# Layer 0's convolution and MLA branches and output product as three fp32r passes, MLA heads in step

## The reference

```
def _merge_branches(pt, ys, p):
    g_a, g_b, g_c = jnp.split(jax.nn.sigmoid(pt[10]), 3, axis=-1)
    return (g_a * ys[0] + g_b * ys[1] + g_c * ys[2]) @ p['w_out']

def _attend(qn, qr, kn, kr, v):            # MLA: 8 heads, 128 + 64 wide
    s = (einsum('bhqd,bhkd->bhqk', qn, kn) + einsum('bhqd,bkd->bhqk', qr, kr)) * MLA_SCALE
    return einsum('bhqk,bhkd->bhqd', softmax(s), v)

def _trunk_layer(...):
    parts = split((x * (1 + scale1) + shift1) @ w_in + b_in)
    y = merge(gla(parts), attend(...) @ mla_wo, conv_module(parts) @ conv_wo)
    x = layer_norm(DN_ALPHA * x + gate1 * y)
    x = layer_norm(DN_ALPHA * x + gate2 * conv_ffn(x * (1 + scale2) + shift2))
```

## Time and profile before

| | us |
|---|---|
| median of three runs | 3217.84 (3217.02 to 3219.92) |
| the profiled execution | 3218.65 |
| its span | 3216.8 |
| PE busy | 3022.4 |
| DVE busy | 1681.4 |
| ACT busy | 1160.4 |

### The profile page before, as it was taken

How to read it: one execution, slowest core, us unless ns; L and a number is a source line. 1 busy time by engine, 2 the same in 40 slices (tenths; PEclk the granted TensorE clock), 3 DMA queues, 4 the chain that set the end, 5 groups by cost and what they waited for, 6 DMA issues and landing times.

```text
span 3216.8 us, 40794 instructions
## 1 busy us (share of the span) xinstructions
PE 3022.4 (94%) x16475; PEld 2287.7 (71%) x16475; DVE 1681.4 (52%) x2885; ACT 1160.4 (36%) x1911; POOL 273.6 (9%) x146
## 2 busy tenths in 40 slices
PE   6989899999998989999999999999999899898998
PEld 3666554444444468877588866789988898897997
DVE  4148867642221177753538882249753644545554
ACT  2033420133231153332323133347555444434444
POOL 2000000000000000000000000000020333320442
PEclk8999999999999999999999999999999999989999
DMA  6223324322323222332223442245652564432562
GB/s 210 79 66 92 92 66 153 122 69 92 104 93 119 90 79 92 99 93 73 89 56 92 126 113 79 92 144 191 177 174 66 151 179 143 143 100 76 166 176 91
DMA packets 419325, 362.38 MB, mean 113 GB/s; under 512 B 20229, under 2 KB 392550, under 8 KB 419140
## 3 DMA queue, kind: packets, MB, share of 16 engines
q1 hardware_dynamic: 416928, 359.11, 36.1%
q10 hardware_dynamic: 1028, 0.39, 0.0%
q0 software_dynamic: 1184, 0.28, 0.0%
HBM read 358.70 MB, written 1.05 MB: 112 GB/s over the span
## 4 chain that ended last, share of the span: by engine, by line
PE 79%; DVE 9%; ACT 5%; issue 4%; DMA 2%; POOL 0%; SPq 0%; POOLq 0%; DVEq 0%; ACTq 0%
PE banks L1037 16%; PE banks L878 7%; PE banks L827 7%; PE banks L910 6%; PE banks L912 5%; PE banks L911 5%; PE banks L901 3%; PE banks L1293 3%; PE banks L1284 3%; DVE conv_out L2503 2%; PE banks L1068 1%; PE banks L1000 1%; ACT narrow_hi L1535 1%; PE banks L1002 1%; PE banks L1001 1%
## 5 line engine op out<-in xcount | busy, mean ns | idle before, releaser
L2293 DVE TENSOR_TENSOR narrow_lo<-wring,narrow_hi 128x1024 fp32r<-128x1024 f32 (+1 forms) x212 | 268.9, 1271 | 379.0 <-ACT narrow_hi L1535 378.8
L910 PE MATMUL banks<-operand_narrow,narrow_hi 128*128 128x256 f32 x1312 | 392.3, 299 | 39.7 <-DVE operand_narrow L2825 20.7
L1535 ACT ACTIVATE narrow_hi<-wring 128x1024 fp32r<-128x1024 f32 (+2 forms) x312 | 309.0, 998 | 223.4 <-PE banks L912 139.7
L911 PE MATMUL banks<-operand_narrow,narrow_hi 128*128 128x256 f32 x1312 | 377.0, 287 | 0.0
L912 PE MATMUL banks<-operand_narrow,narrow_lo 128*128 128x256 f32 x1312 | 377.0, 287 | 0.0
L797 POOL TENSOR_TENSOR narrow_lo<-wring,narrow_hi 128x1024 fp32r<-128x1024 f32 x100 | 251.0, 2513 | 1434.1 <-ACT narrow_hi L1535 1434.1
L2503 DVE SCALAR_TENSOR_TENSOR conv_out<-conv_in,vectors,conv_out 128x512 f32<-128x512 f32 (+1 forms) x464 | 286.6, 618 | 15.3
L910 PEld LDWEIGHTS banks<-operand_narrow,narrow_hi 128*128 128x128 f32 x1312 | 257.7, 196 | 49.2 <-issue 27.8
L1037 PE MATMUL banks<-operand_a,wring 128*128 128x512 f32 (+1 forms) x768 | 256.3, 489 | 3.9 <-DMA wring<-in_w_in_dram 3.9
L911 PEld LDWEIGHTS banks<-operand_narrow,narrow_hi 128*128 128x128 f32 x1312 | 257.7, 196 | 1.7
L912 PEld LDWEIGHTS banks<-operand_narrow,narrow_lo 128*128 128x128 f32 x1312 | 257.4, 196 | 0.0
(11 more groups left out here) (376 smaller groups left out, 5795.9 us busy)
## 6 DMA issues: line engine op xcount, KB each, us to landing
wring<-in_w_in_dram SPq DMA_DIRECT2D x52, 1024.0 KB, 5.4
wring<-in_w_ada_dram SPq DMA_DIRECT2D x48, 1024.0 KB, 5.7
wring<-in_ffn_wup_dram SPq DMA_DIRECT2D x44, 1024.0 KB, 5.1
wring<-in_w_ff_in_dram SPq DMA_DIRECT2D x32, 1024.0 KB, 5.4
wring<-in_w_ff_out_dram SPq DMA_DIRECT2D x32, 1024.0 KB, 5.7
wring<-in_ffn_wdown_dram SPq DMA_DIRECT2D x32, 704.0 KB, 4.7
wring<-in_w_in_dram SPq DMA_DIRECT2D x36, 512.0 KB, 5.1
wring<-in_w_in_dil_dram SPq DMA_DIRECT2D x18, 1024.0 KB, 5.0
```

The lines of the kernel that those rows point to most:

```text
L910: pe.matmul(out, wh, a[:, 0:SEQ], start=first, stop=False)
L911: pe.matmul(out, wh, a[:, SEQ:512], start=False, stop=False)
L1535: act.activation(dst, src, f, **kw).then_inc(*inc)
L2293: tt(NL[:, v % 4, 0:kn, :], w, NH[:, v % 4, 0:kn, :].bitcast(F32), ALU.subtract).then_inc(ev("narrow_lo"), 1)
```

## The change

The gates and values of `co0` and `mo0` and the product `wout0`, 40 tiles in all, become units like those of `up0`: three fp32r passes each. For that ACT makes high parts of `AF` (`MXH`, written where `X` lay), of the convolution's output (`COH`), of MLA's output (`MOH`) and of the merged output (`AH`), and DVE the low parts (`MXL`, `COL`, `MOL`, `GLO`). `X` is saved to device memory by a DMA on POOL's queue once `AF` is made, and comes back when the last gate of `mo0` is done. The highs and lows of the weights get slots of their own for each stage (`SLOTS`, `OVERLAP`, `unit_slot`); ACT and DVE make one unit's split and low at each filler tile, in front of which the units counted so far must be done.

In MLA (both layers) units go in pairs of two heads for the same queries. PE writes both `QN` products, then both `QR` products, the one on rows 0 to 63, the other on rows 64 to 127; then come both turnings, the next pair's scores, the fillers, and both values. DVE's order within a pair is: the next pair's softmax, the fillers, then both copies of the values.

`keep_clock` issues products whose result is overwritten: five in front of layer 1's first tiles, four at `kt` in each layer, six in front of `up0`, three or four at `up1`, `sqk` and `dqk`, two at each of the two `ffin`.

```
     def unit_slot(u):
-        return u if u < 3 else (u - 3) % 2
+        branch, mix_out, up = (pl.unit_at[pl.first[name]] for name in ("co0.1", "wout0", "up0"))
+        if u < branch:
+            return 3 + u
+        if u < mix_out:
+            return 6 + (u - branch) % 2
+        if u < up:
+            return 8 if (u - mix_out) % 2 == 0 else 6
+        i = u - up
+        return 9 + i if i < 3 else (i - 3) % 2
...
# POOL
+        pool.wait_ge(ev("operand_a"), KD)
+        pool.dma_start(XD, X[:, :, :].rearrange("p k n -> p (k n)")).then_inc(ev("x_saved"), 16)
+        pool.wait_ge(ev("x_saved"), 16)
+        pool.wait_ge(*done(pl.last("mo0.6")))
+        pool.dma_start(X[:, :, :].rearrange("p k n -> p (k n)"), XD).then_inc(ev("x_back"), 16)
...
# PE
+        def product3(t, hi, lo, ready=None):
+            u = pl.unit_at[t]
+            pe.wait_ge(ev("w_lo"), u + 1)
+            start_tile(t)
+            wh, wl = unit_parts(u)
+            for k in range(KD):
+                if ready:
+                    ready(k)
+                pe.matmul(bank(t), wh[:, k, :], hi(k), start=k == 0, stop=False)
+                pe.matmul(bank(t), wh[:, k, :], lo(k), start=False, stop=False)
+                mm = pe.matmul(bank(t), wl[:, k, :], hi(k), start=False, stop=k == KD - 1)
+            mm.then_inc(*made(t))
...
+        def keep_clock(t, n):
+            for _ in range(n):
+                pe.matmul(bank(t), cn("ones"), CN[:, 0:512], start=True, stop=True)
...
         # first_tiles(n, ready, *names, idle=0), after arrived / w_lo waits of all its tiles
+            keep_clock(tiles[0][0], idle)
             for k in range(KD):
                 ready(k)
...
             def scores(u):
...
+                for j in range(2):
+                    t, h = F[f"m{l}.s{u + j}"], mla_unit(u + j)[0]
+                    start_tile(t)
+                    pe.matmul(bank(t, 0, nk), QN[:, h, i], KN[:, h, c0:512], start=True, stop=False)
+                for j in range(2):
+                    t, h = F[f"m{l}.s{u + j}"], mla_unit(u + j)[0]
+                    r = slice(64 * j, 64 * j + 64)
+                    mm = pe.matmul(bank(t, 0, nk), QR[h // 2][r, i], KR[r, c0:512], start=False, stop=True)
...
+            start_tile(F[f"kt{l}"])
+            keep_clock(F[f"kt{l}"], 4)
...
-            cols(f"wout{l}", KD, G, n, lambda k: pe.wait_ge(ev("merged_out"), KD * (2 * l + 1) + k + 1))
+                for m in range(KD):
+                    product3(F["wout0"] + m, lambda k: AH[:, k, :], lambda k: GLO[:, k, :],
+                             None if m else lambda k: pe.wait_ge(ev("out_lo"), k + 1))
...
-                first_tiles(n, a_ready(), ("up0", 2))
+                first_tiles(n, a_ready(), ("up0", 2), idle=6)
...
# DVE, after kr0
+            if l == 0:
+                for m in range(KD):
+                    dve.wait_ge(ev("mix_hi"), m + 1)
+                    tt(MXL[:, m, :], AF[:, m, :], MXH[:, m, :].bitcast(F32), ALU.subtract).then_inc(ev("mix_lo"), 1)
+                lows(1)
...
# DVE, MLA
+            softmax(0)
+            for u in range(0, n_units, 2):
+                if u + 2 < n_units:
+                    softmax(u + 2)
+                for name, q in fillers[u // 2]:
                     filler(name, q)
+                if l == 0 and u >= 22 and u % 4 == 2:
+                    mla_low((u - 22) // 2)
+                    mla_low((u - 22) // 2 + 1)
+                value(u)
+                value(u + 1)
...
# DVE, residual after wout0 and the layer norm's end
-                if l == 0 and m == KD - 1:
-                    lows(1)
+                if l == 0 and m:
+                    lows(n_low[0])
...
-                        lows(2)
+                        lows(n_low[0])
+                        lows(n_low[0])
```

More of the change, by code:

```diff
@@ L378, in branch_phase @@
             pl.gemm(f"{name}.{h}", [(cols_chunk(wo if h % 2 else win, (0 if h % 2 else c0) + h // 2 * 256), 2)],
+                    split=lambda i: name in ("co0", "mo0"),
                     after=(lambda j: ada_slot(name[:2] == "wo" and j)) if name[2:] == "0" and (name != "co0" or h)
@@ L828, in parts, with branch_split, conv_split, mla_split @@
             mm.then_inc(*made(t))
+        def product3(t, hi, lo, ready=None):
[10 more added lines that the diff above has]
+            mm.then_inc(*made(t))
+        def branch_split(name, hi, lo, ready, halves):
+            for half in halves:
+                for j in range(2):
+                    t = F[f"{name}.{half}"] + j
+                    if half % 2:
+                        product3(t, hi, lo, ready if half == 1 and j == 0 else None)
+                    else:
+                        product3(t, lambda k: MXH[:, k, :], lambda k: MXL[:, k, :],
+                                 (lambda k: pe.wait_ge(ev("mix_lo"), k + 1)) if name == "co0" and half + j == 0 else None)
+                    if name != "co0" or half:
+                        ada_slot()
+                    yield
+        def conv_split(halves):
+            return branch_split("co0", lambda k: COH[:, conv_tile(k), :], lambda k: COL[:, k, :],
+                                lambda k: pe.wait_ge(ev("conv_lo"), k + 1), halves)
+        def mla_split(halves):
+            return branch_split("mo0", lambda k: MOH[:, k, :], lambda k: MOL[:, k, :],
+                                lambda k: pe.wait_ge(ev("mla_lo"), k + 1), halves)
         def cols_a(name, n, skip=0):
@@ L1229, in mla @@
                 yield
[L1230 to L1236, removed]
+                for j in range(2):
+                    t, h = F[f"m{l}.v{u + j}"], mla_unit(u + j)[0]
+                    pe.wait_ge(*freed(F[f"m{l}.t{u + j}"]))
+                    start_tile(t)
+                    for i in range(nk // P):
+                        mm = pe.matmul(bank(t, 0, P), VM[:, c0 // P + i, h * P:(h + 1) * P],
+                                       PT[:, j, i * P:(i + 1) * P], start=i == 0, stop=i == nk // P - 1)
+                    mm.then_inc(*made(t))
         for l in range(2):
             n = toks(l)
-            first_tiles(512, a_ready(), (f"gr{l}", 1), *([(f"k{l}", 2)] if l else []))
+            first_tiles(512, a_ready(), (f"gr{l}", 1), *([(f"k{l}", 2)] if l else []), idle=5 * l)
             pe.wait_ge(*freed(F[f"gr{l}"]))
@@ L1355, in _ @@
             fillers = mla_fillers(l)
[L1356 to L1359, removed]
+            if l:
+                todo = {"co": branch("co1", CV, n, lambda k: pe.wait_ge(ev("conv_ready"), KD + k + 1), range(1, KD)),
+                        "mo": branch("mo1", B, n, None, (0, 2, 4, 6))}
+            else:
+                todo = {"co": conv_split(range(1, KD)), "mo": mla_split((0, 2, 4, 6))}
+            for pair, _ in enumerate(mla(l)):
+                for name, q in fillers[pair]:
                     next(todo[name])
@@ L1379, in _ @@
             if l == 0:
-                run(narrow_cols("sqk", a_ready(), squares(F["mpre0"])))
+                run(narrow_cols("sqk", a_ready(), squares(F["mpre0"]), 3))
                 row_scale(0)
@@ L1919, in _ @@
                 op(dst, bank(t), ACT.Copy, free(t))
+                if l == 0 and 4 <= i < 10:
+                    conv_high(i - 4)
+                if l == 0 and 10 <= i < 12:
+                    split(i - 8)
+            if l == 0:
+                conv_high(6)
+                conv_high(7)
             n_units = 16 * len(sets[l])
@@ L1964, in _ @@
                      {5: lambda: narrow(up1, 0), 6: lambda: narrow(up1 + 1, 0), 7: lambda: narrow(up1 + 2, 0)} if l else
-                     {6: lambda: split(up), 7: lambda: split(up + 1)})
+                     {m: lambda: split(n_split[0]) for m in range(1, KD)})
             if l:
@@ L2666, in _ @@
             n_units = 16 * len(sets[l])
+            if l == 0:
+                for m in range(KD):
+                    dve.wait_ge(ev("conv_hi"), m + 1)
+                    tt(COL[:, m, :], CV[:, m, :], COH[:, conv_tile(m), :].bitcast(F32), ALU.subtract)\
+                        .then_inc(ev("conv_lo"), 1)
+                    if m == 5:
+                        lows(3)
             def maxima(u):
```

176 lines of the change are left out of this document (119 added, 57 removed).

## The result

The changed kernel takes 3163.26 us (median of four runs, 3161.41 to 3167.2), against 3217.43 for the kernel before in the same comparison: a ratio of 0.9833, 95% interval 0.9816 to 0.985. Forecast were 3161, range 3126 to 3198. The profiled execution took 3165.07 us, its span is 3163.2; that is 53.6 less than the profiled execution of before, where 56.9 were forecast. One later execution, the one that was profiled of the run with the dummies in front, was disturbed (3435.46 us at a mean granted clock of 0.83), so no row of that run is read.

What follows compares the result with a forecast made beforehand. PE was taken as the bound: busy 94% of the span, carrying 79% of the chain. Gains of MLA, mo0, wout0 and smaller terms, less losses at up0 and gr1, sum to -56.9 us: 3161 from the median, range 3126 to 3198.

Steps and rivals of the forecast that it cites:

- The passes: 40 tiles as three fp32r passes: 5.44 us each, saving 1.43 a tile beside nothing, 1.62 in the MLA stage.
- MLA of layer 0: Layer 0's MLA stage: paired heads and cheaper filler tiles, less new waits for value copies; 34 us gained (25 to 55).
- unit of 256 keys: Layer 0's MLA: PE time of one unit at 256 keys before the change, put at 1.96 us.
- up0's start: Between wout0 and up0's body: late weight lows, then six dummies behind that wait; 15.5 us lost (14.5 to 18.5).
- layer 1's first tiles: Layer 1's start (gr1): five dummies stand behind the chunk wait, costing 6.6 us and saving 2.3; 4 us lost.
- kt: Four dummies fill 3.4 us of a 5.40 us hole in each layer: 2 us gained per layer, 4 together.
- `co0`'s first two tiles: Cheaper passes save 2.9 us, but PE waits about 2.8 for the first low: 0 (bounds -3 and +4).
- The MLA of layer 1: Eight 64-row products vanish (8.4 us), a first pair's softmax costs about 2.4: 6 us gained (bounds -9 and +8).
- Covered waits: Rival: waits for value copies in layer 0's MLA pairs are covered, 21.5 us more gained, 3140; chance 0.16.
- A fallen clock: Rival: PE's clock falls after the MLA pairs' waits, 3.1 us at each of 15 pairs, 3208; chance 0.08.
- The dry ring: Rival: late slot release makes 11 MLA-stage weight chunks each cost a wait and half clock, 86 us lost, 3248; chance 0.05.
- No gain in the passes: Rival: with lows or loads between them tiles stay near 6.87 us, 57 us not gained, 3219; chance 0.03.

Runs made afterwards that it cites:

- the run with all three: Changed kernel plus up0's weight lows made early, dummies of two starts before their waits, value copies before lows in layer 0's MLA: 3124.11 us, ratio 0.9725.
- the run with the products apart: Changed kernel with each head's 64-row score product again following its own 128-row product: 3195.51 us, ratio 0.9946 to the kernel before.

## Why the prediction was right

**The passes.** 1.4 us a tile came out: wout0 43.7 us for 54.95, eight tiles. In the MLA stage it was 1.41 too (7.06 less 5.65), not 1.62. The values of `mo0` take 47.9. The wait of 4.70 for weights is gone there; that it is gone because the ring slots are now freed by the low was not tested by itself. (A tile is 24 matmuls in its three passes; the 48 in the prediction's signs is a slip.)

**MLA of layer 0, -28.9 for -34.** The idle time is as counted: 240 - 213.8 = 26.2 us in the window, forecast 21.5 + 4.5. The order of DVE as its cause is shown by the run with the values first. That the waits sum to 21.3 for 21.5 is partly luck. Three of the 14 hold 5.5 us that the prediction did not count: a table load of 1.28 us on ACT in front of a sigmoid (the wait before 897.68), the lows of two finished heads, 1.20 us each time (before 911.69 and 946.07), and 1.83 us for which ACT waits for a late chunk (before 946.07). The chain behind that last one, the longest:

```profile
936.94 5.16 DMA wring<-in_w_in_dram
942.13 1.06 ACT branch_w_hi L1640
943.29 1.23 DVE branch_w_lo L2443
944.51 1.20 DVE mla_out_lo L2836 x2
```

The missing 5 us are busy time, 213.8 for 207.8: a filler tile takes 5.65 on the mean of 22 and not 5.44, since its first products, behind other shapes, come slower than 0.227 (4.6 us together; at 803.66 the second follows the first after 0.34), and one pair's scores ran at half clock, 1.6 us. The step that was mis-sized is the filler's price, which I had taken from up0's unbroken row of tiles. The prediction's unit of 256 keys, 1.96, is a slip too: its own terms add up to 1.88, 1.4 us less over the eight pairs.

**up0's start, +16.0 for +15.5, and layer 1's first tiles, +4.3 for +4.** Both causes are shown by edits: the first by the lows made early alone (16 us back), the second by the dummies in front of the wait, read in the run with all three (6.3 back).

**The small ones.** kt gave more than taken, 3.3 and 3.6 for 2 each, as the states behind it ran at full clock too. `co0`'s first two tiles gave 0.4 for 0. The MLA of layer 1 gave 4.3 for 6 although a pair saves more than I took (9.9 by the products, 9.3 in the run with them apart): the first softmax and the values behind the merges must then cost 5.0 to 5.6, not 2.4; this split was not measured. X's way out and back took 7.8 and 8.6 us for 2 MB and no instruction waited long for it.

**Not foreseen.** +1.5 us in layer 0's query rotation and +1.4 at the start of `down0`, both with the same waits as before and a lower clock; -1.7 in the same rotation stretch of layer 1, at a higher one. Their causes stay open.

**The total.** 53.6 for 56.9 is nearer than its terms: the MLA stage fell 5.1 short, and 2.8 of what made up for it lie in the first 66 us, ahead of the change. Without these the gain is 50.8.

**The rivals.** Covered waits: no, 21.3 us are there. A fallen clock: once in 15 pairs, 1.6 us. The dry ring: once, in the wait of 3.52 us above, where SP issues the chunk at 936.94, when the low that frees its slot is made; no other split of the MLA stage waits for a chunk. No gain in the passes: no.

## What to carry to other kernels

When a step is made cheap by handing preparation to other engines, read where that preparation stands in their order: here two DVE instructions of 1.2 us at the end of a layer norm cost 16 us, and one in front of a copy cost 18 over 14 waits, with DVE under half busy in both windows (23.72 of 48 us, 90.56 of 240). Products that are to keep the clock up belong in front of the wait that they bridge; behind it they cost their length. Here a price taken from an unbroken row of tiles, 5.44 us, was too low for tiles that are mixed with other shapes, 5.65.

## What the runs showed of the hardware that I had not expected

In these traces the clock after a wait does not follow from the wait's length. The same pair of the MLA stage waits 2.92 us in the changed kernel and in the run with the products apart; first the changed kernel, then the other, eight records of the same product:

```profile
897.68 1.07 PE L1159 MATMUL banks<-consts,probs 128*128 128x128 f32 x8 [2.92 <-DVE mla_qn L2832]
```

```profile
910.43 1.94 PE L1159 MATMUL banks<-consts,probs 128*128 128x128 f32 x8 [2.92 <-DVE mla_qn L2830]
```

1.07 us at full clock, 1.94 at half (granted 1.00 and 0.50, that is 2.4 and 1.2 GHz). Within the changed kernel two waits of 2.26 us:

```profile
801.60 0.63 PE L1159 MATMUL banks<-consts,probs 128*128 128x128 f32 x4 [2.26 <-DVE mla_qn L2832]
802.06 1.03 PE L1307 MATMUL banks<-mla_kn,mla_qn 128*128 128x256 f32 x4
```

```profile
830.47 0.63 PE L1159 MATMUL banks<-consts,probs 128*128 128x128 f32 x4 [2.26 <-DVE mla_qn L2832]
830.93 2.76 PE L1307 MATMUL banks<-mla_kn,mla_qn 128*128 128x512 f32 x4
```

And the longest wait of the stage:

```profile
946.07 1.07 PE L1159 MATMUL banks<-consts,probs 128*128 128x128 f32 x8 [3.52 <-DVE mla_qn L2832]
```

After the first of the two the four records of 256 columns take 1.03 us, at full clock; after the second those of 512 columns take 2.76, where the row at 865.02 above has 1.88. After 3.52 us the clock is still full. In the pair at 830.47 the granted clock fell from 1.00 to 0.50 at 831.80, 1.3 us after PE had gone on; in the one at 910.43 at 909.76, while PE still waited. The Trainium skill, "TensorE: Matmul & The Clock Gate", section "Why this matters for your kernels", says that idle gaps between bursts, from a certain length on, bring the array back to half rate. The rows here do not sort by length: the clock stayed up around the waits of 2.92 us at 897.68 and 3.52 at 946.07 and fell at that of 2.26 at 830.47; in the first pair of the run with the products apart it fell at 735.68, where PE had last waited 1.04 us. So in these traces a wait of 1 to 4 us costs itself, or itself and 1.3 to 5.2 us more (1.6 in the fallen pair here, the rest in the run with the products apart), and its length does not tell which.
